# Latent attention: two banks for the head values, values one turn later, logits in two banks

## The chip, the cores and the metric

The kernel runs on one core of a Trainium2 chip as one program. The metric is the time of one execution on the device in microseconds (us); lower is better. TensorE multiplies into PSUM, which has eight banks of 512 float32 columns by 128 partitions; VectorE and ScalarE read PSUM and write SBUF; GpSimd works in SBUF; SyncE issues the DMAs of the weights.

## The reference

A block of two layers (recurrence, two kinds of attention, feed-forward) is followed by a second block of two layers. The sequence has 512 tokens of width 1024. The change concerns the second block's latent attention (16 heads, queries and keys of 64 + 32 elements, values of 64):

```python
lat = h @ w_in                       # 1024 -> 384 + 256 + 32
q  = (rmsnorm(cq, q_norm) @ w_q_up).reshape(B, S, 16, 96)
kv = (rmsnorm(ckv, kv_norm) @ w_kv_up).reshape(B, S, 16, 128)
q, k = [first 64 | rope(last 32)]    # the key's rope part is shared by the heads
# for each head and each block of 128 queries:
s = jnp.einsum('bhqd,bhkd->bhqk', qi, kt) * 96 ** -0.5   # causal mask
p = softmax(s)
o = jnp.einsum('bhqk,bhkd->bhqd', p, vt)
y = o.reshape(B, S, 1024) @ w_o
```

## The kernel before

Everything is held transposed, features on partitions and the 512 tokens along the free dimension. Large products are made of three matmuls each: an operand is split in a high and a low part (HH and HL, weights whi and wlo), and high times high, low times high and high times low are summed in one bank (lines 420 to 422, in `proj`). Weights stream in as blocks of eight 128x128 tiles. ScalarE makes whi from the raw block (L934), VectorE makes wlo (L1468), both called by `feed` some blocks ahead of TensorE.

Each engine has its own written-out program in the same order of stages, and the order within a stage is the order of the calls. Signals count what an engine has finished. A `Ring` hands out PSUM banks in turn: `take(key, banks)` gives the next bank of the ring, and TensorE first waits for the instructions that freed the bank's last owner (table `freed`).

Latent attention (`mla`) first makes the latents and the values of all heads (VM). Then it runs a loop over turns s. Turn s stands for head h = s // 4 and query block n = s % 4; there are 64 of them, software-pipelined over 68 turns of the loop. What one (h, n) passes through:

- `front(s)` on TensorE (L711): logits of 128 queries by 128(n+1) keys, into a bank of ring `sm` (banks 0, 1, 2). VectorE adds the mask, writes PM and takes the row maximum in one instruction (L1968); this frees the bank. A small multiplication negates the maximum (L1973). ScalarE takes the exponential and the row sum (L1290).
- `norm(s)` on VectorE, one turn later: reciprocal (L1978) and multiplication of the n+1 blocks of PM (L1980).
- `mid(s)`, three turns later: TensorE transposes the n+1 blocks (L719) into a bank of ring `tb_` (3, 4). VectorE (s even, L1988) or ScalarE (s odd, L1299) copies them to PTM, which frees the bank.
- `heads_out(s)`, four turns later on TensorE (L731): n+1 value products into 64 partitions by 128 columns of the bank of the head pair, from ring `ob` (bank 5 alone). A product is two instructions in the profile: "x6" at n = 2. The first call of a pair (n = 0, h even) takes the bank.
- `keep(s)` on ScalarE and VectorE, four turns later, when a pair is complete (s % 8 == 7): ScalarE copies the bank to HH (L1306), VectorE subtracts to make HL (L1735), and that frees the bank.
- `head_proj(h + 1, part)`: queries of the next head in turns with n = 0 (nine matmuls of L420 to L422), keys of the next two heads in turns with n = 1 of odd heads (six). They go to banks 6 and 7. ScalarE copies the first 64 rows (L1276 queries, L1283 keys), VectorE makes the two rotary products of the query (L1940, L1941), and GpSimd adds them (L2273) and copies the shared key rows (L2278).

On TensorE a turn s is front(s), mid(s-3), heads_out(s-4), head_proj. On VectorE it is front(s), norm(s-1), mid(s-3) when that is even, keep(s-4), head_proj. On ScalarE it is front(s), mid(s-3) when that is odd, keep(s-4), head_proj. After the loop the output projection `out_proj("mla")` reads HH and HL, row block by row block, and a ring of all eight banks serves it.

Of the kernel before, what the change touches and what calls it, by code (L numbers as in the profile page):

```python
# [201 lines left out]
def program(nc, xt, wst, mst, crow, vec, cst, trig, oh, tab, wax, out, bvec, lse):  # L202
    with ExitStack() as ctx:
# [190 lines left out]
        def tensor_engine(lane):  # L394
            e = lane.e
            owner, main = {}, [Ring(4, 5, 6, 7)]

            def take(key, banks):
                bank = banks.next()
                for signal, name in freed.get(owner.get(bank), ()):  # L400
                    lane.wait_ge(signal, name)
                owner[bank], bank_of[key] = key, bank
                return ps[:, bank, :]
# [9 lines left out]
            def proj(keys, nk, sh, sl, ready, between=None, ks=None):  # L413
                o = {}
                for k in ks or range(nk):
                    for key in keys:
                        wh, wl, names = weights(1)
                        o[key] = take(key, main[0]) if k == 0 else ps[:, bank_of[key], :]
                        lane.wait_ge(*ready(k))
                        e.matmul(o[key], wh, sh(k), start=k == 0, stop=False)  # L420
                        e.matmul(o[key], wh, sl(k), start=False, stop=False)  # L421
                        ins = e.matmul(o[key], wl, sh(k), start=False, stop=k == nk - 1)  # L422
                        if k == nk - 1:
                            names = names + [key]
                        if names:
                            ins.then_inc(*mm_done.up(*names))
                    if between is not None:
                        between(k)
# [21 lines left out]
            def normed(s):  # L450
                return lambda k: (v_norm, ("hl", s, k))
# [228 lines left out]
            def mla():  # L680
                main[0], norms = Ring(0, 1, 2, 3, 4, 5), Ring(6, 7)
                proj([("lat", m) for m in range(6)], 8, hh, hl, normed(("p", 0, 1)))
                i = 0
                for z, ms in enumerate(lat_sets):
                    o = take(("ln", z), norms)
                    for k, m in enumerate(ms):
                        lane.wait_ge(a_mix, ("lsq", m))
                        ins = e.matmul(o, C["ones"][:], T[i % 3], start=k == 0, stop=k == len(ms) - 1)
                        ins.then_inc(*mm_done.up(("lsq", m), ("ln", z)))
                        i += 1  # L690
                ch, cw = (lambda k: CH[:, k, :]), (lambda k: CW[:, k, :])
                ck, kw = (lambda k: CH[:, 3 + k, :]), (lambda k: CW[:, 3 + k, :])
                for f in range(2):
                    proj_rows([("vm", f, q) for q in range(4)], 2, 4, ck, kw, lambda k: (v_mix, ("cw", 3 + k)))
                main[0], sm, tb_, ob = Ring(6, 7), Ring(0, 1, 2), Ring(3, 4), Ring(5)

                def head_proj(h, part):
                    if part == 0:
                        proj([("mq", h)], 3, ch, cw, lambda k: (v_mix, ("cw", k)))
                    elif part == 1 and h % 2 == 0:  # L700
                        proj([("mk", h // 2)], 2, ck, kw, lambda k: (v_mix, ("cw", 3 + k)))

                def front(s):
                    h, n = s // 4, s % 4
                    q, k, w = QH[h % 3], KH[h % 3], 128 * (n + 1)
                    o = take(("ms", s), sm)
                    lane.wait_ge(a_mix, ("mqh", h))
                    lane.wait_ge(g_done, ("rope", h))
                    lane.wait_ge(a_mix, ("mkh", h))
                    lane.wait_ge(g_done, ("kr", h))  # L710
                    e.matmul(o[:, 0:w], q[0:96, n * 128:(n + 1) * 128], k[0:96, 0:w], start=True, stop=True).then_inc(  # L711
                        *mm_done.up(("ms", s)))

                def mid(s):
                    n = s % 4
                    o = take(("mt", s), tb_)
                    lane.wait_ge(v_mix, ("mp", s))
                    for c in range(n + 1):
                        ins = e.transpose(o[:, 128 * c:128 * c + 128], PM[s % 4][:, 128 * c:128 * c + 128], C["ident"][:])  # L719
                    ins.then_inc(*mm_done.up(("mt", s)))  # L720

                def heads_out(s):
                    h, n = s // 4, s % 4
                    half = 64 * (h % 2)
                    if n == 0 and h % 2 == 0:
                        take(("mo", h // 2), ob)
                    o = ps[:, bank_of[("mo", h // 2)], :]
                    lane.wait_ge(a_mix if n % 2 else v_mix, ("mx", s))
                    lane.wait_ge(a_mix, ("vm", h // 8, 3))
                    for c in range(n + 1):  # L730
                        ins = e.matmul(o[half:half + 64, n * 128:(n + 1) * 128], VM[:, c, 64 * h:64 * h + 64],  # L731
                                       PTM[s % 3][:, 128 * c:128 * c + 128], start=c == 0, stop=c == n)
                    ins.then_inc(*mm_done.up(("mo", s)))

                head_proj(0, 0)
                head_proj(0, 1)
                for s in range(68):
                    if s < 64:
                        front(s)
                    if 3 <= s < 67:  # L740
                        mid(s - 3)
                    if s >= 4:
                        heads_out(s - 4)
                    if s < 60 and s % 4 < 2:
                        head_proj(s // 4 + 1, s % 4)

# [165 lines left out]
        def scalar_engine(lane):  # L912
            e = lane.e

            def bank(key):
                return ps[:, bank_of[key], :]
# [325 lines left out]
            def mla():  # L1242
# [44 lines left out]
                def front(s):  # L1287
                    w, s_ = 128 * (s % 4 + 1), smr[s % 4]
                    lane.wait_ge(v_mix, ("mneg", s))
                    e.activation(PM[s % 4][:, 0:w], PM[s % 4][:, 0:w], ACT.Exp, bias=s_[:, 0:1], scale=MLA_SCALE,  # L1290
                                 accum_out=s_[:, 1:2]).then_inc(*a_mix.up(("me", s)))

                def mid(s):
                    if s % 2:
                        w = 128 * (s % 4 + 1)
                        lane.wait_ge(mm_done, ("mt", s))
                        if s >= 3:
                            lane.wait_ge(mm_done, ("mo", s - 3))
                        e.activation(PTM[s % 3][:, 0:w], bank(("mt", s))[:, 0:w], ACT.Copy).then_inc(*a_mix.up(("mx", s)))  # L1299
                        freed[("mt", s)] = ((a_mix, ("mx", s)),)  # L1300

                def keep(s):
                    if s % 8 == 7:
                        m = s // 8
                        lane.wait_ge(mm_done, ("mo", s))
                        e.activation(HH[:, m, :], bank(("mo", m)), ACT.Copy).then_inc(*a_mix.up(("mh", m)))  # L1306

                head_proj(0, 0)
                head_proj(0, 1)
                for s in range(68):  # L1310
                    if s < 64:
                        front(s)
                    if 3 <= s < 67:
                        mid(s - 3)
                    if s >= 4:
                        keep(s - 4)
                    if s < 60 and s % 4 < 2:
                        head_proj(s // 4 + 1, s % 4)

# [73 lines left out]
            s = ("f", 0, 0)  # L1393
# [51 lines left out]
        def vector_engine(lane):  # L1445
            e = lane.e

            def bank(key):
                return ps[:, bank_of[key], :]
# [464 lines left out]
            def mla():  # L1914
# [76 lines left out]
                def keep(s):  # L1991
                    if s % 8 == 7:
                        m = s // 8
                        keep_low(HL[:, m, :], bank(("mo", m)), HH[:, m, :], a_mix, ("mh", m), ("ml", m))
                        freed[("mo", m)] = ((v_mix, ("ml", m)),)

                head_proj(0, 0)
                head_proj(0, 1)
                for s in range(68):
                    if s < 64:  # L2000
                        front(s)
                    if 1 <= s < 65:
                        norm(s - 1)
                    if 3 <= s < 67:
                        mid(s - 3)
                    if s >= 4:
                        keep(s - 4)
                    if s < 60 and s % 4 < 2:
                        head_proj(s // 4 + 1, s % 4)

# [142 lines left out]
            s, AMB = ("f", 0, 0), small[:, 8:16]  # L2153
# [450 lines left out]
```

## Time and profile before

| | us |
|---|---|
| median of 3 runs | 3756.47 |
| lowest, highest | 3754.92, 3760.41 |
| profiled execution | 3753.44 |
| its span | 3751.6 |
| TensorE matmuls busy | 3599.6 (96%) |
| TensorE weight loads busy | 2888.0 (77%) |
| VectorE busy | 2019.4 (54%) |
| ScalarE busy | 1332.3 (36%) |
| GpSimd busy | 128.5 (3%) |

The span is the time from the first to the last instruction of the profiled execution. An engine's busy time counts its own instructions only; weight loads lie beside matmuls. A number in brackets behind an instruction is how long its engine stood idle before it and which instruction of which engine ended that. The loop of latent attention begins at 1743.2 us of the span, and the output projection behind it at 1913.4 us.

### The profile page before, as it was taken

The numbers are of one execution on the slowest core, as the hardware profiler recorded it, in microseconds if no ns is written. First come the engines' busy times: TensorE is split into PE (matmuls) and PEld (weight loads), VectorE is DVE, ScalarE is ACT, GpSimd is POOL, SyncE is SP. The second block draws the span as 40 slices with busy tenths as digits, with TensorE's granted clock in tenths as the row PEclk, the third lists the DMA queues.
The fourth block names the chain that finished last, engine by engine and source line by source line (L and its number), as shares of the span: only waits on it lengthen the run. The fifth ranks groups of instructions, "written<-read, shape, count | busy, mean of one in ns | idle before, by whom it ended". The sixth has DMA issues, their size and how long they took to land.

```text
span 3751.6 us, 41675 instructions
## 1 busy us (share of the span) xinstructions
PE 3599.6 (96%) x16712; PEld 2888.0 (77%) x16712; DVE 2019.4 (54%) x3608; ACT 1332.3 (36%) x2291; POOL 128.5 (3%) x126
## 2 busy tenths in 40 slices
PE   6899999999999999998999999999999999989998
PEld 5647888766888888885677888888878888868886
DVE  7856756576757654576765235523553333344233
ACT  3563323353423332234443223323324334333222
POOL 3330000000000000001100000000000000000000
PEclk9989999999999999999999999999999999989999
DMA  6314555422555455521012222222222222212231
GB/s 258 107 40 144 197 193 174 141 80 74 180 194 194 151 190 195 192 101 65 29 51 96 96 96 96 85 96 97 95 83 82 75 83 78 62 55 95 96 101 62
DMA packets 155469, 429.09 MB, mean 114 GB/s; under 512 B 45468, under 2 KB 50524, under 8 KB 155277
## 3 DMA queue, kind: packets, MB, share of 16 engines
q1 hardware_dynamic: 155276, 426.45, 33.5%
q8 instruction: 131, 2.15, 0.2%
q14 instruction: 62, 0.50, 0.0%
HBM read 423.98 MB, written 2.40 MB: 114 GB/s over the span
## 4 chain that ended last, share of the span: by engine, by line
PE 85%; DVE 11%; ACT 2%; issue 1%; DMA 0%; POOL 0%; SPq 0%; ACTq 0%; DVEq 0%; POOLq 0%
PE ps L420 25%; PE ps L421 24%; PE ps L422 24%; PE ps L731 1%; PE ps L457 1%; PE ps L711 1%; PE ps L771 1%; PE ps L809 1%; DVE X L1621 1%; DVE mraw L1456 1%; PE ps L796 1%; DVE HL L1520 1%; PE ps L577 1%; DVE TT L1535 1%; PE ps L470 1%
## 5 line engine op out<-in xcount | busy, mean ns | idle before, releaser
L420 PE MATMUL ps<-HH,whi 128*128 128x512 f32 x3168 | 1254.9, 396 | 26.1 <-DVE HL L1520 13.0
L421 PE MATMUL ps<-HL,whi 128*128 128x512 f32 x3168 | 1238.1, 391 | 0.0
L422 PE MATMUL ps<-HH,wlo 128*128 128x512 f32 x3168 | 1238.0, 391 | 0.0
L1468 DVE TENSOR_TENSOR wlo<-wraw,whi 128x1024 fp32r<-128x1024 f32 x526 | 644.1, 1225 | 774.2 <-ACT whi L934 774.0
L934 ACT ACTIVATE whi<-wraw 128x1024 fp32r<-128x1024 f32 x548 | 576.1, 1054 | 693.5 <-PE ps L422 684.6
L420 PEld LDWEIGHTS ps<-HH,whi 128*128 128x128 f32 x3168 | 597.8, 189 | 166.2 <-issue 35.8
L421 PEld LDWEIGHTS ps<-HL,whi 128*128 128x128 f32 x3168 | 597.9, 189 | 126.1 <-issue 4.9
L422 PEld LDWEIGHTS ps<-HH,wlo 128*128 128x128 f32 x3168 | 597.7, 189 | 126.2
L1456 DVE CUSTOM_DVE_ANT_0 mraw<-mraw,CB 128x1024 f32<-128x1024 f32 x224 | 282.3, 1262 | 0.9 <-DMA mraw<-mst 0.9
L1654 DVE TENSOR_TENSOR TT<-TT,ps 128x512 f32<-128x512 f32 x116 | 79.7, 687 | 212.9 <-PE ps L422 182.2
L420 PE MATMUL ps<-PHf,whi 128*128 128x512 f32 x352 | 136.9, 389 | 0.0
L421 PE MATMUL ps<-PLf,whi 128*128 128x512 f32 x352 | 136.9, 389 | 0.0
L420 PE MATMUL ps<-PHa,whi 128*128 128x512 f32 x352 | 136.9, 389 | 0.0
L421 PE MATMUL ps<-PLa,whi 128*128 128x512 f32 x352 | 136.9, 389 | 0.0
L420 PE MATMUL ps<-PHb,whi 128*128 128x512 f32 x352 | 136.9, 389 | 0.0
L421 PE MATMUL ps<-PLb,whi 128*128 128x512 f32 x352 | 136.9, 389 | 0.0
L422 PE MATMUL ps<-PHf,wlo 128*128 128x512 f32 x352 | 136.9, 389 | 0.0
L422 PE MATMUL ps<-PHa,wlo 128*128 128x512 f32 x352 | 136.9, 389 | 0.0
L422 PE MATMUL ps<-PHb,wlo 128*128 128x512 f32 x352 | 136.9, 389 | 0.0
L1011 ACT ACTIVATE TT<-ps 128x512 f32<-128x512 f32 x72 | 43.0, 597 | 236.0 <-PE ps L422 236.0
L977 ACT ACTIVATE HH<-TT,MOD 128x512 fp32r<-128x512 f32 x63 | 45.2, 723 | 117.3 <-DVE TT L1535 117.3
L422 PEld LDWEIGHTS ps<-PHb,wlo 128*128 128x128 f32 x352 | 66.1, 188 | 13.8
(327 smaller groups left out, 3928.4 us busy)
## 6 DMA issues: line engine op xcount, KB each, us to landing
wraw<-wst SPq DMA_DIRECT2D x548, 512.0 KB, 3.3
mraw<-mst SPq DMA_DIRECT2D x224, 512.0 KB, 4.3
MR<-mst SPq DMA_DIRECT2D x16, 512.0 KB, 13.8
X<-xt SPq DMA_DIRECT2D x8, 256.0 KB, 5.1
BB<-bvec SPq DMA_DIRECT2D x8, 256.0 KB, 3.4
TT<-lse SPq DMA_DIRECT2D x16, 128.0 KB, 3.0
out<-X SPq DMA_DIRECT2D x8, 256.0 KB, 2.0
CB<-crow SPq DMA_DIRECT2D x2, 512.0 KB, 4.6
```

Of the source, the lines that this page charges most:

```text
L420: e.matmul(o[key], wh, sh(k), start=k == 0, stop=False)
L421: e.matmul(o[key], wh, sl(k), start=False, stop=False)
L422: ins = e.matmul(o[key], wl, sh(k), start=False, stop=k == nk - 1)
L457: ins = e.matmul(o[:, 4 * j + at_:4 * j + at_ + rhs.shape[1]], src[:, 128 * j:128 * j + 128], rhs, start=first and j == 0, stop=j == 3, sk ...
L470: e.matmul(o, C["ones"][:], T[0] if s[0] == "q" else T[2], start=True, stop=True).then_inc(*mm_done.up(("root", s)))
L577: ins = e.matmul(o[:, 0:n], C["later"][:], sp_[:, off[kt]:off[kt] + n], start=True, stop=kt == 3)
L934: e.activation(whi[:, b % SPLIT, :], wraw[:, b % RAW, :], ACT.Copy).then_inc(*whi_made.up(b))
L977: e.activation(HH[:, m, :], T[m % 5], ACT.Identity, bias=MOD[:, v, m:m + 1]).then_inc(*a_norm.up(("hh", s, m)))
L1011: e.activation(a_, src, ACT.Silu).then_inc(*a_ffn.up(("silu", tag, i)))
L1456: e.tensor_tensor_reduce(out=raw, in0=raw, in1=CB[:], scale=1.0, scalar=0.0, op0=ALU.mult, op1=ALU.add, accum_out=MOD[:, v, j:j + 1]).then ...
L1468: e.tensor_tensor(wlo[:, x % RAW, :], wraw[:, x % RAW, :], whi[:, x % SPLIT, :].bitcast(F32), ALU.subtract).then_inc(*wlo_made.up(x))
L1654: e.tensor_tensor(a_, a_, bank(("u", tag, i)), ALU.mult).then_inc(*v_ffn.up(("au", tag, i)))
```

## The change

The value products of successive head pairs use banks 5 and 2 in turn. Bank 2 comes from the logits, which have two banks in place of three. `heads_out` and `keep` are called five turns after `front` in place of four, in all three engines' programs, and the loop has 69 turns.

```diff
-                main[0], sm, tb_, ob = Ring(6, 7), Ring(0, 1, 2), Ring(3, 4), Ring(5)
+                main[0], sm, tb_, ob = Ring(6, 7), Ring(0, 1), Ring(3, 4), Ring(5, 2)
...
# TensorE
-                for s in range(68):
+                for s in range(69):
                     if s < 64:
                         front(s)
                     if 3 <= s < 67:
                         mid(s - 3)
-                    if s >= 4:
-                        heads_out(s - 4)
+                    if s >= 5:
+                        heads_out(s - 5)
                     if s < 60 and s % 4 < 2:
                         head_proj(s // 4 + 1, s % 4)
...
# ScalarE, and VectorE likewise
-                for s in range(68):
+                for s in range(69):
...
-                    if s >= 4:
-                        keep(s - 4)
+                    if s >= 5:
+                        keep(s - 5)
```

## Rows read from the trace of the kernel before

**Rows 1.** The page: engines, the chain that ended last, TensorE's clock in slices.
```profile
PE 3599.6 (96%) x16712; PEld 2888.0 (77%) x16712; DVE 2019.4 (54%) x3608; ACT 1332.3 (36%) x2291; POOL 128.5 (3%) x126
...
PEclk9989999999999999999999999999999999989999
...
PE 85%; DVE 11%; ACT 2%; issue 1%; DMA 0%; POOL 0%; SPq 0%; ACTq 0%; DVEq 0%; POOLq 0%
```

**Rows 2.** TensorE's windows: length, busy, clock, DMA share, GB/s, one pair of heads.
```profile
1763.00:1784.50 21.50, 19.43 (x102) 1.00 0.08 24
```

**Rows 3.** Waits, 1743 to 1914: waiter, releaser: total us, times, longest.
```profile
PE ps L731 <- DVE HL L1735: 8.9, 7, 1.3
PE ps L731 <- DVE PTM L1988: 6.7, 9, 1.1
PE ps L711 <- POOL KH L2278: 3.0, 1, 3.0
```

**Rows 4.** TensorE's timeline, 1789 to 1796: start, duration, instruction, idle before.
```profile
1789.00 0.60 PE L719 MATMUL ps<-c_ident,PM 128*128 128x128 f32 x4
1790.37 0.87 PE L731 MATMUL ps<-PTM,VM 128*64 128x128 f32 x6 [0.77 <-DVE PTM L1988]
1791.17 1.12 PE L711 MATMUL ps<-KH,QH 96*128 96x512 f32 x2
1792.13 0.27 PE L719 MATMUL ps<-c_ident,PM 128*128 128x128 f32 x1
1792.34 1.09 PE L731 MATMUL ps<-PTM,VM 128*64 128x128 f32 x8
1793.35 0.49 PE L711 MATMUL ps<-KH,QH 96*128 96x128 f32 x2
...
1795.33 0.43 PE L731 MATMUL ps<-PTM,VM 128*64 128x128 f32 x2 [1.27 <-DVE HL L1735]
```

**Rows 5.** The same timeline, VectorE and ScalarE.
```profile
1788.45 0.42 DVE L1968 CUSTOM_DVE_ANT_0 PM<-ps,c_caus 128x256 f32<-128x256 f32 x1
...
1789.18 0.67 DVE L1980 TENSOR_SCALAR PM<-PM,small 128x128 f32<-128x128 f32 x1
...
1789.77 0.54 DVE L1988 COPY PTM<-ps 128x384 f32<-128x384 f32 x1
1790.24 0.54 DVE L1968 CUSTOM_DVE_ANT_0 PM<-ps,c_caus 128x384 f32<-128x384 f32 x1
...
1793.98 0.58 ACT L1306 ACTIVATE HH<-ps 128x512 fp32r<-128x512 f32 x1
1794.59 0.69 DVE L1735 TENSOR_TENSOR HL<-ps,HH 128x512 fp32r<-128x512 f32 x1 [0.64 <-ACT HH L1306]
```

**Rows 6.** Waits of VectorE in one pair of heads, 1784.5 to 1806.
```profile
DVE PM L1968 <- PE ps L711: 1.8, 2, 0.9
DVE QH L1940 <- PE ps L422: 1.8, 1, 1.8
...
DVE wlo L1468 <- ACT whi L934: 1.2, 1, 1.2
...
DVE HL L1735 <- ACT HH L1306: 0.6, 1, 0.6
```

**Rows 7.** Timeline rows of the first head and of the last.
```profile
1760.47 0.60 ACT L1299 ACTIVATE PTM<-ps 128x512 f32<-128x512 f32 x1
...
1763.14 0.50 PE L420 MATMUL ps<-CH,whi 128*128 128x512 f32 x1
...
1904.67 0.29 DVE L1980 TENSOR_SCALAR PM<-PM,small 128x128 f32<-128x128 f32 x1
```

**Rows 8.** Timeline, three projection matmuls in the loop's first turns.
```profile
1744.20 0.44 PE L420 MATMUL ps<-CH,whi 128*128 128x512 f32 x1
1744.44 0.63 PE L421 MATMUL ps<-CW,whi 128*128 128x512 f32 x1
1744.86 0.63 PE L422 MATMUL ps<-CH,wlo 128*128 128x512 f32 x1
```

More of the change, by code:

```diff
@@ L1998, in mla @@
                 head_proj(0, 1)
-                for s in range(68):
+                for s in range(69):
                     if s < 64:
@@ L2005, in mla @@
                         mid(s - 3)
-                    if s >= 4:
-                        keep(s - 4)
+                    if s >= 5:
+                        keep(s - 5)
                     if s < 60 and s % 4 < 2:
```

## The prediction

> **What bounds the kernel now.** I read the page first. TensorE is busy 96% of the span and holds 85% of the chain that ended last [rows 1], so a change pays only where TensorE stands still. The change touches one stage, latent attention (1743 to 1914 us). The windows of that stage say what it loses: a pair of heads takes 21.50 us, of which TensorE works 19.43, with the clock fully granted and the DMA engines 8% busy [rows 2]. Six such stretches stand in a row and read alike within 0.04, so some 2.07 us are lost in each pair. The table of waits names the losses [rows 3]: 8.9 us in 7 waits of the value matmuls (L731) for the low half HL (L1735), 6.7 us in 9 waits of the same line for the copy of the transposed probabilities (VectorE, L1988), and 3.0 us once for GpSimd's key rows, before the loop starts. The timeline places the first two in one pair [rows 4]. At 1790.37 the six value matmuls of a turn have waited 0.77 us; at 1795.33 the first two of a new pair of heads have waited 1.27 us. Together 2.04, which is the 2.07 of the windows. Neither VectorE nor ScalarE is the bound: in the pair from 1784.5 VectorE itself stood 1.8 + 1.8 us waiting for TensorE and 1.2 + 0.6 for ScalarE [rows 6].
>
> **Part 1: values in banks 5 and 2.** Today the values of all head pairs share bank 5. A pair's first value matmul may not start before ScalarE has copied the last pair out (0.58 us at 1793.98) and VectorE has made the low half (0.69 us at 1794.59) [rows 5]; TensorE stands for 1.27 us meanwhile. With two banks the same bank comes back a pair later, 21.5 us against about 1.3, so the wait is gone at all 7 places: 7 x 1.27 = 8.9 us. The copy and the subtraction stay, in the same order on their queues; nothing on TensorE follows them at once. Behind the subtraction on VectorE stand the next logits, the low weights and the rotary products.
>
> **Part 2: values one turn later.** This removes no instruction. In turn s TensorE now issues logits(s), transposes(s-3), values(s-5). Values(s-4) waited for a copy made of the turn just before. Values(s-5) needs a copy that transposes(s-3) must already have waited for, because the transposes alternate over two banks and take the bank that this copy frees. So the wait moves rather than vanishes: it now ends in front of the next transposes, with one logits matmul and the older values ahead of it. Worked at 1789.00 [rows 4]: four transposes take about 0.60, the four value matmuls of turn n=1 about 0.55 (six take 1791.17 - 1790.37 = 0.80), so logits n=3 start near 1790.1 and, taking 1792.13 - 1791.17 = 0.96, end near 1791.1. The copy in question runs 1789.77 to 1790.31 [rows 5]. It is hidden with some 0.8 us to spare. Seven such places give 7 x 0.77 = 5.4 us; an eighth, the 1.1 us of the first turns, I treat separately. If the cover were missing, all of the 5.4 would come back. At the 16 turns that wait for ScalarE's copy, TensorE loses at most a tenth each now (transpose at 1792.13, values at 1792.34); I count 0 and keep 1 us for the upper end.
>
> **Part 3: logits in two banks.** Logits(s) now wait for VectorE's masked maximum (L1968) of turn s-2 instead of s-3. A wait in front of the logits also holds back the transposes, values and projections of that turn. But the transposes that follow need normalised probabilities of s-3, which VectorE makes after the maximum of s-2, so in-order TensorE could not get far without it. Numbers: logits n=3 would start near 1790.1 and need the maximum that ended at 1788.45 + 0.42 = 1788.87; the logits after them would start near 1791.1 + 0.21 + 0.80 = 1792.1 and need the one that ended at 1790.24 + 0.54 = 1790.78 [rows 5]. Slack 1.2 and 1.3 us. I take 0 in the steady pairs. The lower bound is nothing gained, since the third bank shows no wait it alone cures; the upper one is in the rivals.
>
> **Does VectorE keep up?** Per pair it needs 21.5 less its waits for TensorE, 3.6, so 17.9 us, its waits for ScalarE included [rows 6]. TensorE needs 19.43. About 1.5 us per pair are left, and the multiplication L1980 decides how safe that is: 128 columns took 0.67 us at 1789.18 [rows 5] while GpSimd's rotary sum was running, and 0.29 us at 1904.67 [rows 7] when GpSimd was idle. One such collision per head is in the 17.9 already. The Trainium skill (SBUF — State Buffer, "SBUF: two separate sides") says that VectorE and GpSimd take an exclusive lock on a shared port pair for a whole instruction and that the loser blocks. The trace's 0.67 against 0.29 agrees; by that rule shifted collisions with the key copies would cost VectorE further pieces of 0.4 us, which the 1.5 us absorb.
>
> **Start and end.** The first head has a projection at a low clock and a cold pipeline, and VectorE is late there. The fourth transposed block leaves its bank when ScalarE's copy ends, 1760.47 + 0.60 = 1761.07 [rows 7]. In the new order two transposes (half of the four's 0.60) and eight value matmuls (1793.35 - 1792.34 = 1.01) follow, so the projection starts near 1762.4 instead of 1763.14 [rows 7]: 0.7 us gained, bounds 0 and 1.4. After the last projection there are only turns of logits, transposes and values, and VectorE's and ScalarE's chain is nearly as long as TensorE's. Of the last pair's 2.04 I keep 1.3, because one set of transposes will probably stand for ScalarE's copy of two turns before; bounds 0 and 2.04. The added 69th turn brings no instruction: TensorE's last values come in the same order. The output projection reads this pair's HH and HL last (row block 7), some 5 us after they start, so it does not wait.
>
> **Sum.** 0.7 + 6 x 2.04 + 1.3 = 14.2 us, between 8.9 (part 1 only) and 17. The profiled execution took 3753.44 us (span 3751.6 and 1.8 around it); less 14.2 it gives 3739.2. It was 3.0 below the median of the runs, 3756.47, so for a median I say 3742.3. The rest of the program only starts earlier. There the clock may turn out otherwise: TensorE's clock was below full in several slices [rows 1], and in the loop's first turns, after the stand of 3.0 us [rows 3], matmuls started 0.42 us apart (1744.44, 1744.86), the 1.2 GHz level, against 0.24 just before (1744.20, 1744.44), the 2.4 GHz level [rows 8]. Five or so such matmuls cost 1 us; later stages can win or lose one or two such stretches, +-3 us, about the spread of the three runs.
>
> **Rivals.**
> (a) Only the bank wait goes; the turn's delay brings nothing, since the transposes wait for the same copy. For it: the copy frees the bank that the transposes take. Against: 0.8 us of cover. 7 x 1.27 = 8.9, time 3747.6.
> (b) No change to speak of. VectorE is closer to the bound than I think, its order (subtraction, low weights, rotary products, then maximum) pushes the maxima late, and TensorE waits at L711 and L719 for what it used to wait for at L731. For it: VectorE idles 17% of a pair for TensorE only. Against: 17.9 is under 19.43. It would give 0 to -6, about 3754. A sentence apart: the Trainium skill (TensorE: Matmul & The Clock Gate, "HAM oscillation") reports a kernel in which adding PSUM double-buffering "gave no further gain"; by that the time would be 3756. No row here supports it, as the 8.9 us wait stands open in the trace.
> (c) Slower: logits in two banks. TensorE stands at L711 with transposes, values and projections behind it. The point from which it decides is a maximum more than 1.2 us later than now, as it would be if VectorE's rotary products and the low weights of a block came between a turn's logits and its maximum. At 1 us in each of three turns per pair that is 3.0 against 2.04 won: 7 x 0.96 = +6.7, time 3763. Against: the code has both in front of the n=1 maximum only, and the one at 1788.45 already stands behind them [rows 5].
> (d) The change does more: the waits of a tenth go too and VectorE's earlier logits shorten the start. -17 to -19, time 3738.
>
> **How the numbers follow.** Forecast as summed 0.62, (a) 0.14, (b) 0.11, (c) 0.05, (d) 0.08. About 0.2% (7.5 us) is what a measurement of this kernel can tell from no change. Faster by more takes the forecast, (d) and most of (a): 0.82; within it (b) and the rest of (a): 0.13; slower 0.05. The range 3734 to 3752 takes in the forecast with its +-3, (d) and (a), and leaves (c) and most of (b) out.
>
> **What would show it.** Right: no wait of L731 for HL and none of 0.7 us for PTM; a pair of heads 19.4 to 19.6 us; HL starts about 19.5 us apart instead of 21.5; VectorE idle for TensorE about 1.5 us per pair. Wrong: TensorE waits at L711 for PM of L1968 (c), or at L719 for PTM or PM worth 0.5 us or more in each head (a, b); or a pair of about 20.2 us (a). The prediction also falls if later stages change their own length by more than 3 us.

## The result, and the profile after

| | before | after |
|---|---|---|
| median of 5 runs, us | 3754.92 | 3740.34 |
| lowest, highest | 3751.27, 3760.41 | 3738.69, 3740.6 |
| span of the profiled execution | 3751.6 | 3738.8 |
| first logits of the loop | 1743.21 | 1747.32 |
| output projection starts | 1913.44 | 1901.74 |
| loop (difference of the two) | 170.23 | 154.42 |

The ratio of after to before is 0.9954, 95% interval 0.9942 to 0.9967: faster, by 17 us with the interval's 12 to 22. The medians differ by 14.6 us. The forecast was 3742.3 us, 14.2 us less.

The two spans differ by 12.8 us: the loop is 15.8 us shorter, the part behind it 1.1 us shorter (1838.2 to 1837.1), and the part ahead of it 4.1 us longer. The last is not put down to the change, since the code there is the same. Kernels with the same code ahead of the loop reached it between 1743.09 and 1750.90 us in the profiles below. The two profiles agree within 0.1 us up to 643 us of the span; by 928 us they are 4.1 us apart, and they stay so up to the loop. TensorE's granted clock over 783 to 856 us was 0.88 before and 0.81 after (0.77 in two_logit_banks, the latest to reach the loop). So the loop is what the rest of this text compares.

The page after, as in [rows 1]. It hardly tells the two kernels apart: the shares of the chain move by a point, and one slice of the clock, far ahead of the loop, reads 8 in place of 9.

```profile
PEclk9989999989999999999999999999999999989999
...
PE 86%; DVE 10%; ACT 2%; issue 1%; DMA 0%; POOL 0%; SPq 0%; ACTq 0%; DVEq 0%; POOLq 0%
```

One stretch of 19.4 us of TensorE's windows, where [rows 2] had 21.50 with 19.43 busy: the window shows no idle time any more. ScalarE's copy to HH (L1306) of successive pairs starts 19.28 us apart (1776.38, the seventh at 1892.08); before it was 21.50 (1772.48, 1901.49).

```profile
1782.40:1801.80 19.40, 19.40 (x103) 1.00 0.09 28
```

The waits of TensorE in the whole loop, against [rows 3]. L731 has gone from the list; what is left over 1 us in all is the stand for GpSimd's key rows ahead of the loop.

```profile
PE ps L711 <- POOL KH L2278: 3.0, 1, 3.0
PE ps L711 <- DVE small L1968: 0.7, 1, 0.7
PE ps L719 <- ACT PTM L1299: 0.5, 1, 0.5
PE ps L719 <- DVE PTM L1988: 0.3, 1, 0.3
PE ps L719 <- DVE PM L1980: 0.2, 1, 0.2
```

The same head as in [rows 4], TensorE. No bracket is left. The "x6" values (query block n=2) of 1792.67 stand now behind one more transpose, and between the values of 1790.92 and them 1.75 us pass, of which TensorE computes all. The transpose at 1792.47 needs the bank that VectorE's copy frees at 1791.93 (next rows): 0.54 us to spare, where the prediction had worked out 0.8.

```profile
1790.39 0.60 PE L719 MATMUL ps<-c_ident,PM 128*128 128x128 f32 x4
1790.92 0.65 PE L731 MATMUL ps<-PTM,VM 128*64 128x128 f32 x4
1791.50 1.12 PE L711 MATMUL ps<-KH,QH 96*128 96x512 f32 x2
1792.47 0.27 PE L719 MATMUL ps<-c_ident,PM 128*128 128x128 f32 x1
1792.67 0.87 PE L731 MATMUL ps<-PTM,VM 128*64 128x128 f32 x6
1793.47 0.49 PE L711 MATMUL ps<-KH,QH 96*128 96x128 f32 x2
1793.86 0.44 PE L719 MATMUL ps<-c_ident,PM 128*128 128x128 f32 x2
1794.23 1.09 PE L731 MATMUL ps<-PTM,VM 128*64 128x128 f32 x8
```

VectorE in that head, against [rows 5]. The copy at 1791.38 ends at 1791.93, and the maximum at 1792.96 follows the multiplication at once. In the kernel before that maximum had waited 0.90 us for TensorE, which is the first of the rows below.

```profile
1792.33 0.69 DVE L1968 CUSTOM_DVE_ANT_0 PM<-ps,c_caus 128x512 f32<-128x512 f32 x1 [0.90 <-PE ps L711]
```

The changed kernel:

```profile
1790.07 0.42 DVE L1968 CUSTOM_DVE_ANT_0 PM<-ps,c_caus 128x256 f32<-128x256 f32 x1
...
1790.79 0.67 DVE L1980 TENSOR_SCALAR PM<-PM,small 128x128 f32<-128x128 f32 x1
...
1791.38 0.55 DVE L1988 COPY PTM<-ps 128x384 f32<-128x384 f32 x1
...
1792.69 0.35 DVE L1980 TENSOR_SCALAR PM<-PM,small 128x256 f32<-128x256 f32 x1
1792.96 0.68 DVE L1968 CUSTOM_DVE_ANT_0 PM<-ps,c_caus 128x512 f32<-128x512 f32 x1
```

### The profile page after: what moved, and what is told of

It reads as the page before. It is cut to its first block, busy times and chain, and to the rows that moved or that the text cites. A ratio compares the mean times of both kernels' runs of the same rounds, so it can differ in the third digit from the quotient of the medians.

```text
span 3738.8 us, 41720 instructions
## 1 busy us (share of the span) xinstructions
PE 3604.5 (96%) x16712; PEld 2892.5 (77%) x16712; DVE 2018.6 (54%) x3608; ACT 1331.9 (36%) x2291; POOL 128.3 (3%) x126
## 4 chain that ended last, share of the span: by engine, by line
PE 86%; DVE 10%; ACT 2%; issue 1%; DMA 0%; POOL 0%; SPq 0%; ACTq 0%; DVEq 0%; POOLq 0%
PE ps L420 25%; PE ps L422 24%; PE ps L421 24%; PE ps L731 1%; PE ps L711 1%; PE ps L457 1%; PE ps L771 1%; PE ps L809 1%; DVE X L1621 1%; DVE mraw L1456 1%; PE ps L796 1%; DVE HL L1520 1%; PE ps L577 1%; DVE TT L1535 1%; PE ps L470 1%
## 5 line engine op out<-in xcount | busy, mean ns | idle before, releaser
L934 ACT ACTIVATE whi<-wraw 128x1024 fp32r<-128x1024 f32 x548 | 576.1, 1054 | 694.9 <-PE ps L422 686.9
L420 PEld LDWEIGHTS ps<-PHa,whi 128*128 128x128 f32 x352 | 66.1, 188 | 13.7
```

The costliest lines, as they stand in the source:

```text
L934: e.activation(whi[:, b % SPLIT, :], wraw[:, b % RAW, :], ACT.Copy).then_inc(*whi_made.up(b))
```

## Experiments

The table holds all of them. "Pair" is the distance of the first and the seventh start of ScalarE's copy to HH (L1306, L1307 in the fill_start kernels), divided by six; "loop" runs from the first logits to the first matmul of the output projection. Both come from one profile each; pairs repeat within 0.02 us (19.283 and 19.300 in two profiles of the changed kernel). Ratios are to the kernel before in runs on the same chip. In the fill_start kernels a projection has moved ahead of the first logits, so that their "loop" holds less work; the section on them compares a longer stretch.

| kernel | pair | loop | ratio (95%) |
|---|---|---|---|
| before | 21.50 | 170.23 | |
| two_logit_banks | 21.50 | 170.42 | 0.9994 (0.9986 to 1.0003) |
| two_value_banks | 21.48 | 170.08 | 0.9998 (0.9989 to 1.0006) |
| turn_later_only | 19.30 | 155.40 | 0.9965 (0.9951 to 0.9979) |
| whole_change | 19.30 | 154.37 | 0.9963 (0.9951 to 0.9976) |
| vector_extra_1 | 20.23 | 162.12 | 0.9975 (0.9965 to 0.9985) |
| vector_extra_3 | 23.88 | 189.85 | 1.0056 (1.0043 to 1.0068) |
| less_vector_before | 20.83 | 165.55 | one run |
| less_vector_two_value_banks | 20.44 | 163.04 | one run |
| less_vector_after | 19.17 | 152.18 | one run |
| fill_start | 19.27 | 150.71 | 0.9950 (0.9936 to 0.9964) |
| fill_start_turn_only | 19.30 | 151.72 | 0.9943 (0.9931 to 0.9956) |
| fill_start_third_turn_bank | 19.17 | 150.53 | 0.9954 (0.9940 to 0.9967) |

### The parts, one at a time

**two_value_banks**, the banks of the change without the later turn:

```diff
# before.py
-                main[0], sm, tb_, ob = Ring(6, 7), Ring(0, 1, 2), Ring(3, 4), Ring(5)
+                main[0], sm, tb_, ob = Ring(6, 7), Ring(0, 1), Ring(3, 4), Ring(5, 2)
```

> The kernel before with the banks of the change (values in banks 5 and 2, logits in two) but values still four turns behind the logits. My theory (the sum of the prediction: the second bank cures the wait for HL, the later turn cures the wait for PTM): the 7 waits of L731 for HL go, the 0.77 us waits for PTM stay; pair of heads 20.2 us instead of 21.5, loop about 9 us shorter, time about 0.24% below before. Rival (the banks do everything, the turn nothing): pair 19.3 us, loop 16 us shorter. Rival (the second bank only moves the wait, since VectorE still makes HL before the next logits): pair 21.5, no change.

The last rival came true: 170.08 against 170.23 us. The wait for HL went at all seven places and came back elsewhere. Waits of this kernel's loop (waiter, releaser: total us, times, longest):

```profile
DVE PM L1968 <- PE ps L711: 16.6, 17, 2.6
...
PE ps L731 <- DVE PTM L1988: 14.8, 15, 1.4
```

Before, L731 waited 8.9 us for HL and 6.7 for PTM, 15.6 in all; now 14.8 for PTM, 1.1 for ScalarE's part of it. The timeline of the head behind a finished pair shows it. The values at 1793.96 start at once, 1.4 us earlier than [rows 4] has them. VectorE still makes HL before the maximum at 1795.16, then the low weights and the rotary products, and makes its copy only at 1801.43. In the kernel before it made the same copy at 1801.48: its chain has not moved. It holds a wait of 1.18 us for ScalarE's high weights (L934), so that it is not VectorE's work alone. TensorE waits for that copy 1.33 us, where it did not wait before, because it had lost 1.27 us to HL in the same head.

```profile
1793.96 0.43 PE L731 MATMUL ps<-PTM,VM 128*64 128x128 f32 x2
...
1794.55 0.69 DVE L1735 TENSOR_TENSOR HL<-ps,HH 128x512 fp32r<-128x512 f32 x1 [0.64 <-ACT HH L1306]
...
1795.16 0.28 DVE L1968 CUSTOM_DVE_ANT_0 PM<-ps,c_caus 128x128 f32<-128x128 f32 x1
...
1797.41 1.23 DVE L1468 TENSOR_TENSOR wlo<-wraw,whi 128x1024 fp32r<-128x1024 f32 x1 [1.18 <-ACT whi L934]
...
1801.43 0.55 DVE L1988 COPY PTM<-ps 128x384 f32<-128x384 f32 x1
...
1802.03 0.87 PE L731 MATMUL ps<-PTM,VM 128*64 128x128 f32 x6 [1.33 <-DVE PTM L1988]
```

The copy in the kernel before:

```profile
1801.48 0.54 DVE L1988 COPY PTM<-ps 128x384 f32<-128x384 f32 x1
```

**turn_later_only**, the later turn without the banks:

```diff
# after.py
-                main[0], sm, tb_, ob = Ring(6, 7), Ring(0, 1), Ring(3, 4), Ring(5, 2)
+                main[0], sm, tb_, ob = Ring(6, 7), Ring(0, 1, 2), Ring(3, 4), Ring(5)
```

> The changed kernel with the banks of before (values in bank 5 alone, logits in three), values five turns behind the logits. My theory as predicted: the PTM waits go (5.4 us), the 7 waits for HL stay at about 1.3 us each, pair about 20.7, loop 5 to 6 us shorter. Rival: one turn later puts a projection of nine matmuls (about 2.1 us), logits and transposes between the last values of a pair and the first of the next, which covers ScalarE's 0.58 and VectorE's 0.69; then the HL wait goes as well, except at the last pair, where no projection follows, pair 19.3, loop about 15 us shorter, and the second value bank is worth under 1 us.

The rival again: pair 19.30, loop 14.8 us shorter. With one value bank the wait for HL is there once, at the last pair, where no projection follows. Waits of this kernel's loop:

```profile
DVE PM L1968 <- PE ps L711: 4.4, 8, 2.6
...
PE ps L719 <- DVE PM L1980: 1.4, 2, 0.9
...
PE ps L731 <- DVE HL L1735: 0.7, 1, 0.7
```

**whole_change**, unchanged, beside it:

> The changed kernel itself, on the same chip as the others, for comparison: pair 19.28 us, loop 154.4 us, about 0.4% below before under every theory.

It repeats the result (154.37 and 154.42 us). Against turn_later_only the other split of the banks is worth 1.0 us of the loop: 0.8 at the last pair, where the wait for HL goes, and 0.2 in the first turns. In the runs the two can't be told apart (medians 3742.2 and 3742.21).

**two_logit_banks**:

```diff
# before.py
-                main[0], sm, tb_, ob = Ring(6, 7), Ring(0, 1, 2), Ring(3, 4), Ring(5)
+                main[0], sm, tb_, ob = Ring(6, 7), Ring(0, 1), Ring(3, 4), Ring(5)
```

> The kernel before with the logits in two banks instead of three and nothing else. My theory: the third bank is worth nothing in the steady pairs (slack over 1 us), at most 0.7 us in the first turns: 0 to +1 us, pair 21.5. Rival: TensorE stands at L711 for VectorE's maximum with everything of the turn behind it; 0.5 us or more in each head, loop 8 us or more longer.

As expected: 0.2 us, one wait of 0.5 us of L711 in the first turns, nothing in the pairs. This excludes rival (c) of the prediction for the kernel before; for the changed kernel its own list of waits does, which has L711 behind a maximum once, for 0.7 us.

### How much room VectorE has

A product of 32x512 whose result nothing reads is put in front of each head's rotary products, once or three times (the waits on semaphores are left out here):

```diff
# after.py, in rope(), for the heads' queries
+                    for z9 in range(1 if name[0] == "rope" else 0):
...
+                        e.tensor_tensor(T[3][64:96, :], b[64:96, :], TG[64:96, :], ALU.mult).then_inc(
+                            *v_mix.up(("extra", name, z9)))
                     e.tensor_tensor(dst, b[64:96, :], TG[64:96, :], ALU.mult).then_inc(*v_mix.up((name, 0)))
```

> The changed kernel with one further VectorE product of 32x512 (about 0.7 us, result unused) in front of each head's rotary products. My theory: VectorE waits 2.4 us a pair for TensorE, the two additions (1.4 us) go into that: pair 19.3 to 19.4, 0 to 1 us in all. Rival (VectorE is close to the bound, or the logits in two banks pass each delay on): each addition delays TensorE, pair up to 20.7, +5 to +11 us.

> The changed kernel with three further VectorE products of 32x512 per head (about 4.3 us a pair). My theory: 2.4 of the 4.3 us are hidden and 1.9 show in each pair, pair about 21.2, +15 us in all. Rival (the order of VectorE's work sets it, not its sum): each head pays nearly the whole, 4 us a pair, +30 us. Rival (VectorE has far more room than its waits show): under +5 us.

Both theories of mine fell, and the rival of each came near. One addition (1.4 us a pair) lengthens the pair by 0.95, three (4.3) by 4.6. VectorE had at most 0.45 us of room a pair in this place, not 2.4. With one addition the delay reaches TensorE through ScalarE: the exponentials (L1290) wait for VectorE's maxima, ScalarE's copy to PTM stands behind them, and the transposes wait for that copy.

```profile
1797.82 0.44 PE L719 MATMUL ps<-c_ident,PM 128*128 128x128 f32 x2 [0.34 <-ACT PTM L1299]
```

With three additions TensorE waits at L711 as rival (c) describes, and its clock falls once in every pair: the granted clock is 0.93 over a pair, where one addition left it at 1.00. The 4.6 us is more than the added work, and the low clock is a cause that it can have; no run sets the two apart. One pair of that loop, and TensorE's waits in all of it:

```profile
1808.49:1832.36 23.87, 21.56 (x101) 0.93 0.07 23
```

```profile
PE ps L711 <- DVE small L1975: 12.0, 15, 2.4
...
PE ps L719 <- DVE PTM L1995: 4.2, 14, 0.3
PE ps L719 <- ACT PTM L1299: 3.3, 7, 0.5
```

Then the other way: the second rotary product is cut from 512 columns to 8 (0.69 to 0.17 us, 1.04 a pair), so that the queries' rotary part is not computed.

```diff
-                    e.tensor_tensor(z[64:96, :], b[96:128, :], TG[96:128, :], ALU.mult).then_inc(*v_mix.up((name, 1)))
+                    wz = 8 if name[0] == "rope" else 512
+                    e.tensor_tensor(z[64:96, 0:wz], b[96:128, 0:wz], TG[96:128, 0:wz], ALU.mult).then_inc(*v_mix.up((name, 1)))
```

> The kernel before with VectorE's second rotary product of each head cut from 512 columns to 8 (about 0.5 us less per head; the queries' rotary part is then not computed). Theory now (TensorE and VectorE wait for each other in turns: values for the copy made one turn before, VectorE's next maximum for TensorE's next logits, so that VectorE's chain is in the period): the pair shortens by 0.5 to 1.0 us from 21.50. Rival (the waits for HL and PTM are two fixed latencies, 1.27 and 0.77, and VectorE's other work lies beside them, as the prediction has it): pair 21.5.

> The same cut in the kernel with two value banks and values four turns behind. Theory: its pair (21.48) is VectorE's chain through both heads, so both cuts of 0.5 us show: 20.4 to 20.6. Rival: pair 21.5, the second bank's wait is held by something other than VectorE.

> The same cut in the changed kernel. Theory: its pair (19.28) is TensorE's own work but for about 0.1 us, so the cut brings at most 0.1 to 0.2 us a pair, in spite of the fact that added VectorE work costs at once. Rival (VectorE's chain is still the bound): 18.3 to 18.6.

All three came as the theory had them: the pair falls by 0.67, 1.04 and 0.12 us. In the kernel before, two thirds of the cut show; with two value banks all of it (1.04 of 1.04), so there VectorE's chain through both heads is the pair; in the changed kernel almost none, so there TensorE's own work is. The waits of L731 over four pairs (1780 to 1860) show the two heads apart. The kernel before with the cut:

```profile
PE ps L731 <- DVE HL L1735: 5.1, 4, 1.3
...
PE ps L731 <- DVE PTM L1989: 1.0, 4, 0.3
```

and the one with two value banks and the cut:

```profile
PE ps L731 <- DVE PTM L1989: 4.3, 8, 0.8
```

In the first, the wait for PTM falls from 0.77 to 0.25 us and the wait for HL stays at 1.27. In the second, both waits for PTM, one in each head, fall by 0.52 (0.77 to 0.25, 1.33 to 0.82). So in the kernel before one head waited for VectorE's chain, and in the other the wait for HL stood in the place of the same wait. The 0.12 us that the cut still brings in the changed kernel lay in TensorE's busy time, not in a wait that its windows show; the third transpose bank below ends at the same 19.17. The changed kernel stands within 0.5 us a pair of both bounds.

### Further than the change

**fill_start** calls the projection of head 1 ahead of the first logits, on three engines:

```diff
# after.py
                 head_proj(0, 0)
                 head_proj(0, 1)
+                head_proj(1, 0)
                 for s in range(69):
...
-                    if s < 60 and s % 4 < 2:
+                    if 0 < s < 60 and s % 4 < 2:
```

> The changed kernel with the query projection of head 1 called before the first logits on TensorE, ScalarE and VectorE instead of behind them, so that it fills the 3.0 us in which TensorE stands for GpSimd's key rows (L2278). Theory: nine matmuls move into the stand, which now precedes the loop; the stretch from the end of the key projection to the first projection of head 3 shortens by 2.5 to 3.5 us, and the 1.2 GHz stretch behind the stand does not come; time 0.1% below the changed kernel. Rival: VectorE and ScalarE are what the first turns wait for; the projection's time is given back as waits of L711 and L719 in the first two heads, gain under 1 us.

From the last matmul of the key projection to the output projection it takes 154.29 us (1747.58 to 1901.87), the changed kernel 157.80 (1743.94 to 1901.74): 3.5 us less, the upper end of what was expected. The stand of 3.0 us is filled by nine matmuls behind a stand of 1.04. They start 0.23 us apart; the changed kernel makes the same ones after the stand, 0.42 us apart from 1748.50 on. Part of what the rival expected came too: the wait of L711 for a maximum in the first turns grew from 0.71 to 1.18 us. TensorE's timeline, fill_start first:

```profile
1747.58 0.39 PE L422 MATMUL ps<-CH,wlo 128*128 128x512 f32 x1
1749.00 0.47 PE L420 MATMUL ps<-CH,whi 128*128 128x512 f32 x1 [1.04 <-DVE TT L1943]
...
1750.23 0.39 PE L422 MATMUL ps<-CH,wlo 128*128 128x512 f32 x1
1750.46 0.40 PE L420 MATMUL ps<-CH,whi 128*128 128x512 f32 x1
```

and the changed kernel:

```profile
1747.32 0.46 PE L711 MATMUL ps<-KH,QH 96*128 96x128 f32 x2 [2.99 <-POOL KH L2278]
...
1748.50 0.63 PE L420 MATMUL ps<-CH,whi 128*128 128x512 f32 x1
1748.92 0.63 PE L421 MATMUL ps<-CW,whi 128*128 128x512 f32 x1
```

TensorE's windows there (length, busy, granted clock, DMA share, GB/s), fill_start and then the changed kernel:

```profile
1749.00:1751.20 2.20, 2.20 (x10) 1.00 0.00 0
```

```profile
1748.50:1752.50 4.00, 4.00 (x11) 0.63 0.14 15
```

**fill_start_turn_only** is the same with one value bank and three logit banks, and **fill_start_third_turn_bank** with `Ring(0, 1), Ring(3, 4, 2), Ring(5)` for logits, transposes and values.

> The same with the banks of before (one value bank, three logit banks) and values five turns behind. If the second value bank is worth nothing in the steady pairs: within 1 us of fill_start, a little less in the first turns (no wait of L711 for the maximum) and 0.5 to 1 us more at the last pair. If it is worth 1.3 us a pair: about 9 us slower than fill_start.

> The changed kernel with the projection of head 1 called first (as in fill_start) and bank 2 given to the transposes (three banks) in place of the values (one bank). Theory: the waits of L719 for copies (0.5 + 0.3 us in the first head, tenths in the pairs) go, the wait for HL at the last pair (0.7 us) is back: from the end of the key projection to the output projection 154.3 to 155.3 us, against 154.3 in fill_start. Rival (each tenth of a wait for a freed transpose bank holds the whole chain): pair 19.0, 2 us shorter.

The same stretch takes 155.29 and 154.09 us. The first is 1.0 us over fill_start, as expected. The second lies 0.2 us under its expected 154.3 to 155.3, with a pair of 19.17, not the rival's 19.0. Medians are 3738.04, 3736.27 and 3735.72 us, all under the 3740.34 and 3742.2 of the changed kernel. The ratios' intervals overlap with one another and with the change's, so that the runs alone prove none of them faster; what the profiles show is 3.5 us in this stage.

## Why the prediction was right, and where it was not

- **Where the time was.** Right. The stage lost 2.07 us a pair in waits of L731; the pair fell by 2.22. The rest of 0.15 lay in TensorE's busy time, which fell from 19.43 to 19.28 us: from a turn's four transposes to the values behind them it was 0.60 us (1801.48 to 1802.08) and is 0.53 (1800.80 to 1801.33). These are the tenths that the prediction counted as 0 and kept for the upper end, and that rival (d) counted as won.
- **Part 1, the second value bank, 8.9 us.** Wrong as put. The step that failed is "the wait is gone at all 7 places: 7 x 1.27 = 8.9 us". The wait did go, but two_value_banks gains 0.15 us of loop, since TensorE then waited for the copy of VectorE, whose chain had not moved. With the later turn it is worth 1.0 us. I had summed two waits as if each were lost time of its own. In truth both stood in one cycle: TensorE waited for a copy made the turn before, and VectorE's next maximum waited for TensorE's next logits (0.90 us in the same head; 16.7 us in all before, 16.6 with two value banks, 3.6 in the changed kernel and 4.4 with the later turn alone). I had read that wait as proof that VectorE had room. The prediction lists what stands behind the subtraction on VectorE and did not follow it to the next copy.
- **Part 2, one turn later, 5.4 us.** The mechanism was right, the size was not: alone it brings 14.8 us. It loosens the cycle, and it also hides the wait for HL, since a projection, logits and transposes now lie between a pair's last values and the next pair's first. That follows from the new order and could have been read off it.
- **Part 3, logits in two banks, 0.** Right: +0.2 us alone.
- **VectorE's room, 1.5 us a pair.** Wrong. Its waits for TensorE are still 2.4 us a pair, 2.2 of them at one place, ahead of the rotary products. Room there can't be used by work that comes behind: with one further product behind it the wait is still 2.2 us (8.9 us over four pairs), and that product cost 0.95 of its 1.4 us. It went well because VectorE's chain still fitted under 19.28 us a pair, by 0.45 us at most and not by 1.5; that it sufficed was luck, and rival (b) had VectorE's nearness right. The slow multiplication stayed as it was: 0.67 us at 1790.79 beside GpSimd's sum; no run here varied it.
- **Start, 0.7 us.** From the first logits to the projection of head 3 it was 19.93 us (1743.21 to 1763.14) and is 19.65 (1747.32 to 1766.97): 0.3. L711 waits once for a maximum there, 0.7 us, but the third logit bank would not have given it back: turn_later_only, which has it, waits at L719 instead and takes 19.70.
- **End, 1.3 us.** What is left of 15.8 after 0.3 and six times 2.22 is 2.2 us, slightly more than the bound of 2.04.
- **Sum.** 0.3 + 13.3 + 2.2 = 15.8 for the forecast's 14.2. The total came out because both waits end, whichever part ends them: the two parts' shares were 0.15 and 14.8 us, not 8.9 and 5.4. Rival (a), which kept the bank's share and dropped the turn's, had it the wrong way round. The right total is therefore no proof of the parts.
- **The signs.** No wait of L731 for HL or PTM is left, as forecast. The pair of 19.28 us lies a little under the forecast 19.4 to 19.6, and VectorE's idle time for TensorE, 2.4 us a pair, lies over the forecast 1.5. None of the signs of being wrong came: no L719 wait of 0.5 us in each head, and the part behind the loop moved by 1.1 us.
- **The rest of the program** moved by up to 8 us ahead of the loop between profiles of kernels that have the same code there. Most of it arises between 643 and 928 us, where the granted clock differs (0.88, 0.81 and 0.77 over 783 to 856 us, in order of arrival at the loop). What lowers it in one execution and not in another was not tried.

## What to carry to other kernels

Two waits on one engine are not two gains. Where engine A waits for B and B in the same stretch for A, take one wait away alone, or follow the chain behind it, before adding them up; here, distance in the software pipeline between a producer and its consumer loosened the cycle, while a further buffer alone moved the wait. Idle time of an engine is room only for work that can be done in that idle time: where it lies in the order counts, not its sum.

## What was not expected of the hardware

Filling the stand of 3.0 us in front of the loop saved 3.5 us, though TensorE's idle time from the key projection to the output projection fell by only 1.6 us (4.8 to 3.2). Most of the rest, about 1.7 us as an estimate from the windows (4.00 us at 0.63 and the 1.20 us ahead of them at 0.83), is the clock: behind the stand of 2.99 us the granted clock was 0.63 over 4 us, with matmuls 0.42 us apart (the 1.2 GHz level), and behind the stand of 1.04 us it was 1.00, with matmuls 0.23 us apart (the 2.4 GHz level). Over the whole of its loop, 1749 to 1902 us, fill_start was granted 1.00. The length of the stand alone does not tell where a low stretch comes. It is 2.46 us in the three less_vector kernels: in less_vector_after the clock fell right behind it (0.63 over 1748 to 1752 us), in less_vector_before it was 1.00 for 8.4 us behind it and fell to 0.57 over 1753 to 1757 us, and the third went like the second. No run varied the stand by itself.
